# One block of a two-block sequence model: compression steps inside dense stages, retention heads inside four gate blocks, rotation partners by DMA

## The reference, cut to what matters

```
h = rmsnorm(x)
q,kc,vc,ks,vs,kw,vw,nsa_g, rq,rk,rv,rg, gate_a,gate_b = split(h @ w_in)
q,kc,ks,kw = rotary(first 16 of each 64 dims);  rq,rk = rotary(all 128 dims)
# NSA, 8 heads in 2 groups of width 64
blk   = windows of 32 positions, stride 16 (31 of them), + position table
k_cmp = silu(blk(kc) @ ck_w1) @ ck_w2 ;  v_cmp = silu(blk(vc) @ cv_w1) @ cv_w2
p_c   = softmax(q k_cmp^T masked) ;  o_c = p_c v_cmp
o_s,o_w = causal softmax attentions on ks,vs and kw,vw
nsa   = sig(g0)*o_c + sig(g1)*o_s + sig(g2)*o_w
# retention, 4 heads of width 128, no softmax
o     = ((rq rk^T) * decay) rv ; o = o * rsqrt(mean(o^2)) ; ret = silu(rg) * o
mix   = sigmoid(gate_a)*(nsa @ w_proj_a) + sigmoid(gate_b)*(ret @ w_proj_b)
x     = x + mix @ w_out ; x = x + relu(rmsnorm(x) @ w_up)^2 @ w_down
```

## Time and profile before

| | before |
|---|---|
| median of 3 runs | 2244.96 us (2243.27 to 2247.13) |
| profiled execution, its own time | 2242.02 us |
| its span | 2240.2 us |
| PE busy | 2108.6 us, 94% |
| PEld busy | 1692.7 us, 76% |
| DVE busy | 1227.6 us, 55% |
| ACT busy | 812.1 us, 36% |
| DMA, mean rate | 83 GB/s |

### The profile page before, as it was taken

The page is one execution under the profiler, slowest core; times in us unless marked ns, Lnnn a source line. Parts: engine busy times, 40 slices in busy tenths (PEclk is TensorE's granted clock), DMA queues, the critical chain, the costliest instruction groups (busy, mean ns, idle before and its releaser), DMA issues. The chain is left out here.

```text
span 2240.2 us, 26341 instructions
## 1 busy us (share of the span) xinstructions
PE 2108.6 (94%) x9974; PEld 1692.7 (76%) x9974; DVE 1227.6 (55%) x1752; ACT 812.1 (36%) x1235; POOL 8.5 (0%) x23
## 2 busy tenths in 40 slices
PE   7878888999999999999999999999998899999997
PEld 6645666888888888877778888878785577888885
DVE  5576434445543446555677474665535647747465
ACT  4156113443221224135344242332425734424242
POOL 0000000000000000000000000000000000000000
PEclk9879998999999999999999999999999999999998
DMA  4200211232222222231212322221220022222221
GB/s 169 96 1 20 94 47 57 84 112 94 95 103 103 94 94 94 85 113 57 94 57 94 113 94 94 85 104 66 94 94 19 1 94 75 84 104 95 96 95 52
DMA packets 33355, 185.88 MB, mean 83 GB/s; under 512 B 4040, under 2 KB 8296, under 8 KB 13680
## 3 DMA queue, kind: packets, MB, share of 16 engines
q1 hardware_dynamic: 31440, 180.46, 22.7%
q0 software_dynamic: 672, 2.11, 0.3%
q10 hardware_dynamic: 1152, 2.10, 0.3%
HBM read 182.54 MB, written 2.11 MB: 82 GB/s over the span
## 5 line engine op out<-in xcount | busy, mean ns | idle before, releaser
L318 ACT ACTIVATE w_hi<-w_raw 128x2048 fp32r<-128x2048 f32 (+3 forms) x174 | 314.4, 1807 | 822.7 <-PE bank L386 714.4
L384 PE MATMUL bank<-a_hi,w_hi 128*128 128x512 f32 x1376 | 537.5, 391 | 7.1 <-PEq L1406 2.1
L386 PE MATMUL bank<-a_hi,w_lo 128*128 128x512 f32 x1376 | 536.2, 390 | 0.0
L385 PE MATMUL bank<-a_lo,w_hi 128*128 128x512 f32 x1376 | 536.2, 390 | 0.0
L332 DVE TENSOR_TENSOR w_lo<-w_raw,w_hi 128x2048 fp32r<-128x2048 f32 (+3 forms) x174 | 374.9, 2156 | 151.4 <-ACT w_hi L318 151.2
L384 PEld LDWEIGHTS bank<-a_hi,w_hi 128*128 128x128 f32 x1376 | 258.8, 188 | 62.7 <-issue 5.4
L386 PEld LDWEIGHTS bank<-a_hi,w_lo 128*128 128x128 f32 x1376 | 258.7, 188 | 53.9
L385 PEld LDWEIGHTS bank<-a_lo,w_hi 128*128 128x128 f32 x1376 | 258.8, 188 | 53.1
L384 PE MATMUL bank<-big_halves,w_hi 128*128 128x512 f32 x616 | 240.5, 390 | 3.4 <-DVE w_lo L332 3.4
L386 PE MATMUL bank<-big_halves,w_lo 128*128 128x512 f32 x616 | 239.9, 389 | 0.0
L385 PE MATMUL bank<-big_halves,w_hi 128*128 128x512 f32 x616 | 239.9, 389 | 0.0
(11 more groups left out here) (338 smaller groups left out, 2457.6 us busy)
## 6 DMA issues: line engine op xcount, KB each, us to landing
w_raw<-in_w_fu SPq DMA_DIRECT2D x44, 1024.0 KB, 4.8
w_raw<-in_w_up SPq DMA_DIRECT2D x16, 1024.0 KB, 4.8
w_raw<-in_w_down SPq DMA_DIRECT2D x16, 1024.0 KB, 4.8
w_raw<-in_w_fd SPq DMA_DIRECT2D x16, 1024.0 KB, 4.8
w_raw<-in_w_mix SPq DMA_DIRECT2D x8, 1024.0 KB, 4.7
w_raw<-in_w_fd SPq DMA_DIRECT2D x8, 768.0 KB, 4.3
w_raw<-in_w_rqk SPq DMA_DIRECT2D x4, 1024.0 KB, 4.8
w_raw<-in_w_rvg SPq DMA_DIRECT2D x4, 1024.0 KB, 4.7
```

The costliest lines, as they stand in the source:

```text
L318: act.activation(w_hi[slot][:, cols], raw[slot][:, cols], ACT.Copy).then_inc(hi_half_ready.sem if half == 0 else hi_ready.sem, 1)
L384: pe.matmul(out, w[0], x[0], start=first, stop=False)
L385: pe.matmul(out, w[0], x[1], start=False, stop=False)
L386: return pe.matmul(out, w[1], x[0], start=False, stop=last)
```

## The change

The first block becomes stages of one list that goes on into the mixing, the network and the mLSTM (one `run`). The code of part 2 is cut into functions that PE, DVE and ACT call inside `kcvc`, `vg` and `rqk`. `attention` now returns its three engine functions instead of opening a Block. The permutation matmuls are gone: POOL copies partner rows with DMAs (SBUF to SBUF) into a cleared buffer, and DVE rotates whole groups of tiles with three instructions. `mix` is cut into `gate` (the first four gate blocks, inside which the four retention heads run), `proj` (their four projection blocks) and `mix` (the other eight, alternating as before). The four gates are kept in SBUF (`sigs`). Number and size of the dense matmuls are unchanged.

```diff
-         "rvg": (4, [(4, 512)]), "mix": (16, [(KT, 256), (4, 256)]), "out1": (4, [(KT, 256)])}
+         "rvg": (4, [(4, 512)]), "gate": (4, [(KT, 256)]), "proj": (4, [(4, 256)]), "mix": (8, [(KT, 256), (4, 256)]),
+         "out1": (4, [(KT, 256)])}
...
+        def rotate(dve, x, swapped_x, cos, sin):
+            like = list(x.shape)
+            dve.tensor_tensor(x, x, cos[:, None, :].broadcast_to(like), ALU.mult)
+            dve.tensor_tensor(swapped_x, swapped_x, sin[:, None, :].broadcast_to(like), ALU.mult)
+            dve.drain()
+            return dve.tensor_tensor(x, x, swapped_x, ALU.add)
...
+            def partners(pool, n, dst, src):
+                for base in (0, 64):
+                    for a, b in ((0, 8), (8, 0)):
+                        pool.dma_start(dst[base + a:base + a + 8], src[base + b:base + b + 8]).then_inc(swapped[n].sem, 16)
...
+            def swaps(pool):
+                pool.wait_ge(pool_step.sem, b_pool + 3)
+                pool.wait_ge(evacuated.sem, e_q + 3)
+                partners(pool, 0, k_swapped[:, 0:1, :], qk[:, 4:5, :])
+                partners(pool, 1, q_swapped[:, :, :], qk[:, 0:4, :])
+                pool.wait_ge(evacuated.sem, e_q + 4)
+                partners(pool, 2, k_swapped[:, 1:3, :], qk[:, 6:8, :])
+                pool.memset(blk[:, :, :, :, NC:CB], 0.0).then_inc(pool_step.sem, 1)
...
+            stages.append(dense("kcvc", two_chunks(a_tiles), scaled_to(qk[:, 4:8, :]), kcvc_late,
+                                between={(0, 8): positions_turned, (1, 12): halves_swapped}))
+            stages.append({"sync": large_loads})
...
+            stages.append(dense_rows("vg", evac_dve=take_rows, late_dve=lambda dve, b, slot, m: rotate_one(dve, 1 + b),
+                                     late_act=lambda act, b, slot, m: hidden_act(act) if b == 0 else None, between={(0, TT - 1): hidden}))
...
+            stages.append(dense("rqk", two_chunks(a_tiles), scaled_to(rqk), rqk_late_dve, none, rqk_late_act, ahead_act=ahead_act, ahead_dve=ahead_dve,
+                                between={(0, 2): hidden_turned, (0, 6): keys, (0, 10): compressed_values, (1, 1): scores,
+                                         (2, 1): probs_turned_pe, (2, 8): outputs}))
...
+            def transfers(pool):
+                pool.wait_ge(out_ready.sem, b_att)
+                for n, dst, src in ((3, swapped_q, qk[:, 0:4, :]), (4, swapped_k, qk[:, 4:8, :])):
+                    for a, b in ((0, 64), (64, 0)):
+                        pool.dma_start(dst[a:a + 64], src[b:b + 64]).then_inc(swapped[n].sem, 16)
...
+            def values(pe, n):
+                pe.wait_ge(weighted.sem, b_w + TT * (n + 1))
+                pe.wait_ge(out_done.sem, b_od + n)
...
+            for n in range(RH):
+                do(3 * n + 1, scores, n, score_order[0:3])
+                do(3 * n + 2, scores, n, score_order[3:4])
+                do(3 * n + 3, values, n)
+            do(12, turn, 0)
+            do(13, turn, 1)
+            do(15, turn, 2)
+            stages.append(dense("gate", two_chunks(a_tiles), gate_early, gate_late_dve, none, gate_late_act, ahead_act=gate_ahead_act,
+                                ahead_dve=gate_ahead_dve, between=at_quarter))
...
+            first = dense("proj", [both], lambda dve, b, slot, m: mixed_dve(dve, b, slot, sigs[b], m["prod"] + b + 1),
+                          lambda dve, b, slot, m: low_mix(dve, b), none, lambda act, b, slot, m: high_mix(act, b), between=begin)
```

More of the change, by code:

```diff
@@ L510, in tensor @@
                     first_pair()
-                if spec.blocks > 2:
+                if any(b > 1 for b, n in between):
+                    for b in range(2, spec.blocks):
+                        by_chunk(b, b % 2, True)
+                elif spec.blocks > 2:
                     with pe.Fori(1 if own else 0, spec.blocks // 2) as i:
@@ new lines, in values @@
+                def values(c, u):
+                    p = u // TT
+                    pe.wait_ge(probs_copied.sem, b_c + c * (2 * U) + (2 * u + 2))
+                    pe.wait_ge(out_done.sem, b_d + (c if together else c * 2 + (p - 1)))
+                    out = out_bank[0 if together else p]
+                    vals = v_of(0, p) if static else v_st[p]
+                    for j in range(TT):
+                        for e in range(2):
+                            rows = slice(64 * e, 64 * e + 64)
+                            last = pe.matmul(out[rows, j * P:S], vals[:, j, rows], turned_keys(p, e, j),
+                                             start=j == 0 and not (together and p == 1),
+                                             stop=j == TT - 1 and not (together and p == 0))
+                    last.then_inc(out_ready.sem, 1)
@@ L1754, in mlp @@
+            mixed.n += 3 * KT
+            gated.n += 4
+            mix_ready = lambda k: ((mixed.sem, b_mix + 3 * k + 2), (mixed.sem, b_mix + 3 * k + 3))
+            add_dve, split_dve, split_act, count, b_sum, ready = add_and_split(lambda k: gain(1, k))
+            third = dense("out1", two_chunks(mix_tiles), add_dve, split_dve, none, split_act, tile_ready=mix_ready)
+            count()
+            return [first, second, third], b_sum, ready
         def mlp(rows, spare, h_hi, h_lo, b_sum, ready):
@@ new lines, in build @@
+        tables = [region(6336 + S * n, S) for n in range(2)]
+        sigs = [work4[:, 0:2, :], work4[:, 2:4, :], region(5120, 2, S), region(5120 + 2 * S, 2, S)]
+        stages = first_projections(o, vg, gate, tables)
+        stages.append(nsa(o, vg, gate))
+        more, *begin = retention(o, tables, sigs)
+        stages += more
+        flat = [region(2 * (S + 2) * r, 2 * (S + 2)) for r in range(4)]
+        rows = [x[:, 0:2 * S].rearrange("p (c s) -> p c s", s=S) for x in flat]
+        u, z = [x[:, :].rearrange("p (c s) -> p c s", s=S + 2) for x in flat[0:2]], rows[2:4]
```

1271 lines of the change are left out of this document (653 added, 618 removed).

## The result

| | before | after |
|---|---|---|
| median (runs) | 2246.05 us (4; 2243.27 to 2247.20) | 2180.26 us (4; 2175.64 to 2180.92) |
| profiled execution | 2242.02 us | 2175.64 us |
| its span | 2240.2 us | 2173.6 us |
| mean granted clock | 0.971 | 0.985 |

The ratio of the times is 0.9713, with a 95% interval of 0.9701 to 0.9724: 65.8 us less, where 66.8 were forecast. The forecast of 2178 was 2 us too low.

The account below looks back on a forecast made before the run. PE was taken to set the end: 123.4 us outside dense products and `attention`, less 41.4 of inserted PE work, 12.7 of waits and 2.5 unseen, gave 66.8 us gained, so 2178 us; range 2165 to 2198.

Parts of the forecast that it names:

- swap matmuls: Partners of kc and vc, still made on PE by two 512-column fp32 matmuls: 2 x 1.02, overlapped 1.8 us.
- pieces in `rqk`: Compression's scores, outputs, transposes, keys and values inserted in `rqk`: 9.0 us of PE time at full clock.
- wait, `kcvc`: PE waits about 1 us at tile 12 of block 1: chain of 9.6 us against 8.2 us after block start.
- `proj`: Waits for halves of retention's heads 2 and 3 (about 1.3 us) and of block 1 (0.6): 1.9 us.
- unseen: Allowance of 2.5 us for waits of 0.2 to 0.5 us at some 20 meeting points.
- 123.4: Time in us before the change, from end of `kcvc` to start of `mix`, that is neither dense product nor `attention`.
- The landing of the kc partners: In `kcvc`, POOL's partner transfers taken to land in 4 us, bounds 2.5 to 12.0; their own queue passes the loads.
- Rival 1: Partners land late, 12.0 us, behind the two 2 MB loads: 8 us more at `kcvc`, gain 56, 2189 us; chance 0.12.
- Rival 2: Retention's chain paces `gate`: three heads wait 4 us each, the hidden layer another 4; gain 51, 2194 us; chance 0.15.
- Rival 3: Clock of filled stages `vg`, `rqk`, `gate` falls to 1.2 GHz, 10.9 us more per block, up to 2295 us; chance 0.03.
- Rival 4: Change doesn't do what it says: compression stays outside, half of its 48 us, 2202 us; chance 0.04.
- the part behind the column sum: Sign: everything behind `out1` stays unchanged to 1 us; the prediction is wrong if that part moves.

Follow-up runs that it names:

- `no_ret`: The changed kernel without retention's scores, weighting, values, square root, gating and transposes, a probe that leaves work out: 2160.31 us, ratio 0.9621 to the kernel before.
- `comp_alone`: The changed kernel with compression, from hidden layer to outputs, in its own stage between `vg` and `rqk`: 2199.37 us, ratio 0.9808 to the kernel before.
- `ret_alone`: The changed kernel with the four retention heads in their own stage between `rvg` and `gate`, scores one head ahead: 2187.76 us, ratio 0.9751 to the kernel before.
- `loads_later`: The changed kernel with the two 2 MB hidden-layer weight loads issued only once the kc tile's partners have landed: 2175.78 us against 2178.41 unaltered.
- `again_b`: The changed kernel measured once more without any edit, as the level of its set: 2178.41 us, ratio 0.9715 to the kernel before.

## Why the prediction was right

**The ledger closes.** Terms as forecast, and as measured:

| | forecast | measured |
|---|---|---|
| swap matmuls | 1.8 | 2.8 (62.36 to 65.12) |
| hidden layer | 9.7 | 10.2 busy |
| pieces in `rqk` | 9.0 | 10.8 (60.87 - 43.8 - 6.3 of `vg`) |
| retention | 20.9 | 20.4 (205.53 - 185.12) |
| wait, `kcvc` | 1.0 | 3.42 |
| waits, hidden layer | 1.5, 0.8 | 1.53, 0.45 |
| before and after `attention` | 3.3, 1.4 | 3.66, 1.18 |
| `rvg` | 1.3 | 0.94 |
| `gate` | 1.5 | 1.53 |
| `proj` | 1.9 | 0 |
| unseen | 2.5 | 0.9 |
| `attention` | 0 | 1.2 more |
| sum | 56.6 | 59.0 |

123.4 - 59.0 = 64.4 us, and the stretch to the column sum is 65.0 shorter. "Unseen" is what is left of 25.55 us of idle time without `attention`'s own 84.64 - 72.68 and the seven waits. The premise, that inserted work costs its PE time alone, is shown by `no_ret`; that what left the lonely stretches was waiting and half clock, by `comp_alone` and `ret_alone`. These two put back 19.1 and 7.5 of the 65.8 us. No run puts back the rotations with the permutation matrix, the rope tables and the silu of rg in stretches of their own (leftovers of 12.0, 12.80 and 14.06 us in the reckoning of before); that their time left is read from the ledger and not shown by an experiment.

**What was mis-sized.** The landing of the kc partners: 4 us taken, 5.7 measured, inside my bounds of 2.5 to 12.0. I argued that POOL's own queue keeps them clear of the loads. It doesn't quite: `loads_later` shows 1.8 us where no load runs beside them. The trace of before had a hint: of the eight transfers behind the 3.4 us of the earlier trace rows, seven landed in 3.2 to 3.6 us, and the one of 5.1 us was issued at 1026.10, 0.2 us behind a load. Most of what else made the wait 2.4 us too long is a gap of 0.65 us between the end of the take-out (51.62) and POOL's first issue (52.27), which my chain left out, and that 9.6 - 8.2 is 1.4, where I entered 1.0.

Behind the wait the clock was halved, so that the swap matmuls took 2.05 and 1.66 us, not 1.02 each. This goes with the wait: the fall stands in seven of the nine profiles with a wait of 2.8 to 3.6 us there (not in `again_b` and `comp_alone`) and in none of the three without it.

**What was luck.** The terms that were too small add to 7.3 us (`kcvc`'s wait 2.4, pieces in `rqk` 1.8, `attention` 1.2, swap matmuls 1.0, hidden layer 0.5, before `attention` 0.4); those that were too large add to 4.9 (`proj` 1.9, unseen waits 1.6, retention 0.5, `rvg` 0.4, the hidden layer's waits 0.3, after `attention` 0.2). So the sum is off by 2.4 only because they nearly cancel. The spans agree even more closely with the forecast, 66.6 us against 66.8, and this is luck too: 66.8 - 2.4, and 0.6 that the ledger doesn't place, - 1.1 ahead of `kcvc`'s second block, + 2.7 behind the column sum, where nothing was forecast.

**The rule on the queues.** Of the two rules of the Trainium skill, that on the queues (DMA: Bandwidth & Descriptors, SWDGE vs HWDGE vs iDMA: each engine goes round-robin between them) agrees with 5.4 us rather than 12.0; it lets small transfers pass, but not for nothing.

**The rivals.** Rival 1 (landing) happened in small, 2.4 us of its 8. Rival 2 (retention's chain paces `gate`) did not: one wait of 1.53 us in four heads, at the place forecast. Rival 3 (1.2 GHz in filled stages): `gate` and `rvg` stand at 1.00, but `rqk` loses 1.7 to 3.4 us at the end of the scores or behind them in half of the executions, so its mechanism exists, at a small part of its price. The Trainium skill's rule (TensorE: Matmul & The Clock Gate, A second HAM failure mode: psum-queue depth-cycling) speaks of short idling between groups; here PE's last idle time before the fall is 0.26 us, some 13 us earlier, so no run bears it out for this place. Rival 4 did not happen: compression's pieces stand inside `rqk` in PE's timeline above.

**The tests I named.** `gate` took 64.9 us for its four blocks (66 forecast); the mix's last eight blocks end 54.4 us ahead of the column sum as before, at 435.7 (433). PE's idle time outside `attention` from 60 to 430 us is 8.25 + 4.27 = 12.5 (bound 20). PEclk is 1.00 through `gate`, PE waits 1.53 us before the hidden layer (bound 2), and no matmul with the permutation stands in `rvg`. Four failed. PE waits 3.42 us at kc's rotation, over the bound of 2, and the clock is halved behind it, so that PEclk is 0.98 from 60 us to `attention` and not 1.00. `attention` starts at 151.5, not 144: 1.1 for the later start of the block, 2.4 for the wait, 1.0 for the swaps, 0.5 and 1.8 for the hidden layer and the pieces in `rqk` (which I had scaled from half clock by exactly two), 0.4 before `attention`; the rest is the dense products, some of them at half clock. From there to 435.7 nearly 5 us came back: 1.9 in `proj` and about 1.9 of unseen waits that I had charged and that did not occur, 1.1 of smaller terms, and 1.3 by which the mixing's dense products run faster at PEclk 1.00 (185.12 us in `no_ret`) than before at 0.99 (186.45), less 1.2 more in `attention`. And the part behind the column sum moved by 2.7 us where I had allowed 1; I had named this as a sign of being wrong. Its idle time is 56.95 and 56.70 us, the same; its busy time differs by 2.45 at a clock of 0.98 and 0.99, and with the same code the four unaltered profiles take from 1683.4 to 1685.7. So the bound was tighter than this part repeats, and the sign said nothing on the mechanism.

## What to carry to other kernels

Where one engine sets the pace in dense stages and stands still in a chain between them, put the chain inside: its price is its own time on that engine at the full clock, and that price can be summed beforehand from the trace. First pipeline the chain by itself (retention got half of its gain so), and don't count on borders between program parts (0.3 to 1.0 us each for the three tried here). A small transfer on the path wants its neighbours checked, not only its queue: hold large loads that have time back until it has landed, or do the step on the bound engine if 1 us of it buys 4.

## What the runs showed of the hardware

- The same four 16 KB copies inside SBUF landed in 5.4 us beside two 2 MB loads of another queue and in 1.8 us ahead of them (one profile). The loads took 14.4 and 21.2 us after, 9.4 and 14.8 before, and still 12.2 and 19.7 where they started behind the kc partners. So these four copies are at most a small part of what slows them; the rest stays open.
- TensorE's clock fell to 1.2 GHz with PE busy for every microsecond, at the end of 64 narrow instructions of 32 columns or right behind them, in five of ten executions of the same code.
- 18 executions of one kernel spread over 9 us, in step with the mean granted clock: some 1.6 us for 0.001.
